# A two-layer mixture-of-experts encoder: overflow tiles in mid-stream, expert pairs across groups, ten early gathers and five late

## Time and profile before

| | us |
|---|---|
| median of three runs (1248.49 to 1252.61) | 1248.56 |
| the profiled execution, its own time | 1249.58 |
| its span in the trace | 1247.7 |
| TensorE busy, in the span | 1062.6 (85%) |
| VectorE, ScalarE, GpSimd busy | 492.1, 294.1, 269.7 |

### The profile page before, as it was taken

How to read it: one execution, slowest core, us unless ns; L and a number is a source line. 1 busy time by engine, 2 the same in 40 slices (tenths; PEclk the granted TensorE clock), 3 DMA queues, 4 the chain that set the end, 5 groups by cost and what they waited for, 6 DMA issues and landing times.

```text
span 1247.7 us, 14600 instructions
## 1 busy us (share of the span) xinstructions
PE 1062.6 (85%) x5342; PEld 620.7 (50%) x5342; DVE 492.1 (39%) x1075; ACT 294.1 (24%) x631; POOL 269.7 (22%) x289
## 2 busy tenths in 40 slices
PE   6999999999997898887774998988987998877870
PEld 5777777775455333333223776754545333333320
DVE  3144444435347211111115699996455111111116
ACT  3233232323110111000012455546111010000012
POOL 2000000001000321111033388870003121111033
PEclk9999999999997999989996999999997998999995
DMA  8963222411806899999984293100028999999974
GB/s 274 386 200 112 95 75 71 117 58 58 353 24 264 309 419 421 420 420 421 421 324 120 57 374 97 34 16 9 34 101 309 415 420 421 420 420 420 419 274 133
DMA packets 110287, 303.68 MB, mean 243 GB/s; under 512 B 18440, under 2 KB 65672, under 8 KB 86521
## 3 DMA queue, kind: packets, MB, share of 16 engines
q1 hardware_dynamic: 87977, 254.74, 53.0%
q0 software_dynamic: 22256, 48.22, 10.7%
HBM read 278.34 MB, written 57.12 MB: 269 GB/s over the span
## 4 chain that ended last, share of the span: by engine, by line
PE 52%; DMA 20%; issue 11%; DVE 10%; ACT 2%; POOL 2%; another core or an unknown queue 1%; SPq 1%; DVEq 0%; POOLq 0%
PE bank L541 10%; DMA ring<-in_w_up 10%; PE bank L1234 10%; DMA arena<-in_w_up 8%; PE bank L440 7%; PE bank L1253 6%; PE bank L568 4%; DVE bank L1763 3%; PE bank L591 2%; PE bank L607 2%; PE bank L632 2%; PE bank L1223 1%; PE bank L973 1%; POOL ring L1191 1%; PE bank L348 1%
## 5 line engine op out<-in xcount | busy, mean ns | idle before, releaser
L1234 PE MATMUL bank<-ring,work 128*64 128x512 f32 x704 | 166.1, 627 | 28.4 <-DMA ring<-in_w_up 26.6
L1253 PE MATMUL bank<-ring,work 128*64 128x512 f32 x528 | 126.7, 624 | 28.7 <-DVE work L1272 21.7
L541 PE MATMUL bank<-arena,ring 128*128 128x288 f32 x512 | 131.9, 412 | 0.3 <-issue 0.3
L1549 PE MATMUL bank<-arena,work 128*128 128x288 f32 x512 | 126.6, 410 | 5.7 <-DMA work<-in_w_pw 4.4
L1268 DVE TENSOR_TENSOR work<-work,bank 128x256 f32<-128x256 f32 x33 | 13.9, 421 | 283.8 <-ACT work L1264 276.3
L1234 PEld LDWEIGHTS bank<-ring,work 128*64 128x64 f32 x704 | 57.9, 144 | 134.3 <-issue 132.2
L1549 PEld LDWEIGHTS bank<-arena,work 128*128 128x128 f32 x512 | 98.1, 192 | 33.5 <-issue 4.9
L1712 POOL TENSOR_TENSOR ring<-ring 128x606 f32<-128x606 f32 x76 | 103.6, 1364 | 43.6 <-ACT ring L1660 34.1
L541 PEld LDWEIGHTS bank<-arena,ring 128*128 128x128 f32 x512 | 94.9, 190 | 32.9 <-issue 8.2
L440 PE MATMUL bank<-ring,arena 128*128 128x512 f32 x224 | 99.1, 595 | 2.6 <-ACT arena L1696 2.6
L1234 PE MATMUL bank<-arena,work 128*64 128x512 f32 x352 | 85.6, 642 | 18.4 <-DMA arena<-in_w_up 16.2
(11 more groups left out here) (262 smaller groups left out, 1330.9 us busy)
## 6 DMA issues: line engine op xcount, KB each, us to landing
ring<-in_w_down SPq DMA_DIRECT2D x32, 2048.0 KB, 24.0
ring<-in_w_gate SPq DMA_DIRECT2D x20, 2048.0 KB
ring<-in_w_up SPq DMA_DIRECT2D x20, 2048.0 KB
arena<-in_w_gate SPq DMA_DIRECT2D x10, 2048.0 KB
arena<-in_w_up SPq DMA_DIRECT2D x8, 2048.0 KB
ring<-in_w_qkv SPq DMA_DIRECT2D x24, 512.0 KB, 6.0
y_sorted<-gain POOLq DMA_DIRECT2D x8, 1536.0 KB, 5.7
work<-in_w_pw SPq DMA_DIRECT2D x16, 512.0 KB, 5.8
```

The source lines that it names most:

```text
L541: mm = nc.tensor.matmul(bank[b][:, 0:HT], wa[s][:, w, c, :], xt[:, c, h * HT:(h + 1) * HT], start=c == 0, stop=c == C - 1)
L1234: mm = nc.tensor.matmul(bank[2 + s][rr, :], rows_t[:, c, rr], wgu[g][:, :, e, c, :], start=c == 0, stop=c == C - 1)
L1253: mm = nc.tensor.matmul(bank[5 + h][rr, :], hts[:, c, rr], wdn[s][:, e, c, h * HALF:(h + 1) * HALF], start=c == 0, stop=c == FC - 1)
L1549: mm = nc.tensor.matmul(bank[banks[h][w]][:, 0:GT], wp[s][:, w, c, :], xt[:, c, h * GT:(h + 1) * GT], start=c == 0, stop=c == C - 1)
```

```diff
...
+        y_early = [ring[:, 1, n % EARLY_BUFS * D:(n % EARLY_BUFS + 1) * D] for n in range(2 * TILES)]
+        y_late = [ring[:, 0, j * D:(j + 1) * D] for j in range(TILES)]
...
+        OVER_AT = EPAIRS // 2
+        LAST_SLOT = 2
+        def gu_at(p):
+            if p == EPAIRS - 1:
+                return LAST_SLOT
+            return (p if p < OVER_AT else p + 1) % GU_SLOTS
...
-                do(V.tensor_tensor(grouped(kept), grouped(le), pen[0:r, :].unsqueeze(2).to_broadcast([r, GROUPS, PER_GROUP]),
+                do(V.tensor_tensor(placed_at(kept), grouped(le), pen[0:r, :].unsqueeze(2).to_broadcast([r, GROUPS, PER_GROUP]),
...
+            FAR = float(2 * SLOTS)
+            do(V.tensor_scalar(late_is[:], slot_f[:], float(EARLY_PAIRS * P), None, ALU.is_ge))
+            do(V.scalar_tensor_tensor(late_is[:], slot_f[:], float(EXPERTS * CAP), late_is[:], ALU.is_lt, ALU.mult))
+            do(V.scalar_tensor_tensor(early_slot[:], late_is[:], float(ZERO_ROW), slot_f[:], ALU.mult, ALU.max))
+            do(V.scalar_tensor_tensor(far_f[:], late_is[:], -FAR, slot_f[:], ALU.mult, ALU.add))
+            do(V.tensor_tensor(far_f[:, 0, :], far_f[:, 0, :], far_f[:, 1, :], ALU.min))
+            do(V.tensor_scalar(late_slot[:], far_f[:, 0, :], FAR, None, ALU.add))
...
+                if local == EARLY_PAIRS:
+                    pool.wait_ge(base.gu_mm, i + 1)
+                    for j in range(TILES):
+                        steps.done(pool.memset(y_late[j], 0.0))
+                    pool.wait_ge(further_known, 2 * (l + 1))
+                    pool.wait_ge(over_end, l + 1)
+                    for s in range(2):
+                        pool.wait_ge(base.y_out[s], 16 * (EPAIRS // 2) * (l + 1))
+                    g, there = gu_slot(l, EPAIRS - 1)
+                    pool.wait_ge(base.gu_in[g], there)
+                    early_rows_in(pool, l, range(0, FIRST_EARLY))
                 pool.wait_ge(base.y_ev_a, i + 1 + FREE)
                 pool.wait_ge(base.y_ev_d, i + 1 + FREE)
                 rows_out(local)
                 if local == EARLY_PAIRS:
...
-                        for k in range(2):
...
-                                y_rows_in(pool, j, k, early_slot)
...
+                    early_rows_in(pool, l, range(FIRST_EARLY, 2 * TILES))
+        FIRST_EARLY = 2
...
+        def early_rows_in(pool, l, some):
+            for n in some:
+                j, k = n // 2, n % 2
+                if n >= EARLY_BUFS:
+                    pool.wait_ge(early_sum, TILES * l + (n - EARLY_BUFS) // 2 + 1)
+                pool.indirect_dma_start(y_early[n][0:rows[j], :], None, y_sorted,
+                                        bass.IndirectOffsetOnAxis(early_slot[0:rows[j], k, j:j + 1], 0),
+                                        bounds_check=SLOTS, oob_is_err=False).then_inc(gathered[j], 16)
+        def late_pool(pool, l):
             for s in range(2):
                 pool.wait_ge(base.y_out[s], 16 * (EPAIRS // 2) * (l + 1) + 16)
-            pool.wait_ge(extra_end, l + 1)
             for j in range(TILES):
...
-                for k in range(2):
-                    y_rows_in(pool, j, k, late_slot if early(j, k) else slot)
+                pool.indirect_dma_start(y_late[j][0:rows[j], :], None, y_sorted,
+                                        bass.IndirectOffsetOnAxis(late_slot[0:rows[j], j:j + 1], 0),
+                                        bounds_check=SLOTS - 1, oob_is_err=False).then_inc(late_in[j], 16)
+        def early_dve(dve, steps, l, j):
+            r = rows[j]
+            dve.wait_ge(gathered[j], 32 * (l + 1))
+            steps.done(nc.vector.scalar_tensor_tensor(x[0:r, j, :], y_early[2 * j][0:r, :], gate_w[0:r, 0, j:j + 1],
+                                                      x[0:r, j, :], ALU.mult, ALU.add))
+            nc.vector.scalar_tensor_tensor(x[0:r, j, :], y_early[2 * j + 1][0:r, :], gate_w[0:r, 1, j:j + 1],
+                                           x[0:r, j, :], ALU.mult, ALU.add).then_inc(early_sum, 1)
         def combine_dve(dve, steps, l, j):
             r = rows[j]
-            dve.wait_ge(gathered[j], landed(j, l + 1))
-            steps.done(nc.vector.scalar_tensor_tensor(x[0:r, j, :], y_at[0][j][0:r, :], gate_w[0:r, 0, j:j + 1],
...
+            dve.wait_ge(early_sum, TILES * l + j + 1)
+            dve.wait_ge(late_in[j], 16 * (l + 1))
+            nc.vector.scalar_tensor_tensor(x[0:r, j, :], y_late[j][0:r, :], late_gate[0:r, 0, j:j + 1],
                                            x[0:r, j, :], ALU.mult, ALU.add).then_inc(combined, 1)
...
+                if local == OVER_AT:
+                    over_turns(eng, l, over)
...
+            def over(o):
+                act.wait_ge(m.xt_mm, o + 1)
+                nc.scalar.copy(over_xt, bank[7][:].rearrange("p (c r) -> p c r", c=C)).then_inc(m.xt_ev, 1)
+                act.wait_ge(m.gu_mm, o + 1)
+                nc.scalar.activation(over_hid, bank[7][0:CAP, 0:FE], ACT.Silu).then_inc(m.silu, 1)
+                act.wait_ge(m.dn_mm, o + 1)
+                nc.scalar.copy(over_y, bank[7][:]).then_inc(m.y_ev, 1)
+                act.wait_ge(m.y_ev, o + 1 + FREE)
+                for h in range(2):
+                    act.dma_start(y_sorted[dyn(EXPERTS * CAP + o * CAP, CAP), h * HALF:(h + 1) * HALF],
+                                  over_y[h * CAP:(h + 1) * CAP, :]).then_inc(m.y_out, 16)
...
+                if local == EPAIRS - 1:
+                    early_dve(dve, steps, l, 0)
                 ex_y_copy(dve, nc.vector.tensor_copy, base, i, s, k, 1, base.y_ev_d)
...
+                if local == EPAIRS - 1:
+                    for j in range(1, TILES):
+                        early_dve(dve, steps, l, j)
...
+        def of_pair(src, l, p):
+            return src[l].rearrange("(g e) d f -> e g d f", g=GROUPS)[p // 2, 2 * (p % 2):2 * (p % 2) + 2]
...
                 i = EPAIRS * l + local
-                down_first = local >= GU_SLOTS
-                if 0 < local and local + GU_SLOTS < EPAIRS and not down_first:
+                gu = lambda p: gu_load(sp, l, p)
+                late = local in (OVER_AT - 2, OVER_AT - 1, EPAIRS - 3)
+                if 0 < local < GU_SLOTS or late:
                     sp.wait_ge(base.gu_mm, i + 1)
-                    gu_load(sp, l, local + GU_SLOTS)
+                    gu(local + 2 if late else local + GU_SLOTS)
                 if local + 2 < EPAIRS:
                     sp.wait_ge(base.dn_mm, i + 1)
+                    if local == OVER_AT:
+                        sp.wait_ge(m.y_out, 32 * tiles + 32)
+                        sp.sem_inc(over_end, 1)
+                        gu(local + 2)
                     dn_load(sp, l, local + 2, local % 2)
-                if local + GU_SLOTS < EPAIRS and down_first:
-                    gu_load(sp, l, local + GU_SLOTS)
...
+                if local == OVER_AT - GU_SLOTS:
+                    over_loads()
+                elif local >= GU_SLOTS and local + GU_SLOTS < EPAIRS - 1 and not late:
+                    gu(local + GU_SLOTS)
+            m = overs[l]
+            def over_load(o):
+                sp.dma_start(over_x, x_over[dyn(o * CAP, CAP), :]).then_inc(m.x_in, 16)
+                expert = sp.value_load(over_expert[0:1, dyn(o, 1)], min_val=0, max_val=EXPERTS - 1)
+                for w, src in enumerate((w_gate, w_up)):
+                    sp.dma_start(over_gu[:, w, :, :].rearrange("p c f -> p (c f)"),
+                                 src[l, dyn(expert, 1)].rearrange("e (p c) f -> p (e c f)", c=C)).then_inc(m.gu_in, 16)
+                sp.dma_start(over_dn.rearrange("p c n -> p (c n)"),
+                             w_down[l, dyn(expert, 1)].rearrange("e (p c) n -> p (e c n)", c=FC)).then_inc(m.dn_in, 16)
+            def over_loads():
+                sp.sem_inc(m.y_out, 32)
+                with sp.If(tiles > 0):
+                    sp.wait_ge(far_scattered, 16 * (2 * TILES - FAR_FIRST) * (l + 1))
+                    over_load(0)
+                with sp.If(tiles > 1):
+                    with sp.Fori(1, tiles) as o:
+                        sp.wait_ge(m.dn_mm, o)
+                        sp.wait_ge(m.y_out, 32 * o + 32)
+                        over_load(o)
...
-                extra_loads(0)
...
-            sp.wait_ge(gathered[HALF_TILES - 1], landed(HALF_TILES - 1, 1))
+            sp.wait_ge(late_in[HALF_TILES - 1], 16)
...
```

242 lines of the change are left out of this document (104 added, 138 removed).

## The result

The changed kernel takes 1238.86 us (median of 8 runs, 1237.70 to 1239.12), the kernel before 1248.1 (8 runs, 1243.35 to 1252.61). The ratio is 0.9933, 95% interval 0.9917 to 0.9949: faster by 0.67%, some 8.4 us, where 15 were forecast. The profiled execution took 1239.12 us, its span is 1237.5.

What follows compares the result with a forecast made beforehand. Weight streams at 419 to 421 GB/s bound the kernel, with chains of waits at both layer ends. 1249.58 − 4.7 (layer 0) − 10.8 (layer 1) + 0.4 gave 1234.5 us profiled, 1233.5 median; range 1228.5 to 1241.0.

Steps and rivals of the forecast that it cites:

- (1): Layer 0's end: pair 15's store issued 0.3 us later and landing 1.2 later behind more gathers; together +1.5 us.
- they need gathers 0 and 1 within 10.4 us: Tile 0's early sums, ahead of pair 15's output copy, cost nothing if those gathers land by 648.2 us.
- (2): Layer 0, last store's landing to first late sum: 5.98 us down to 3.86, so −2.1.
- (6): Layer 1, last store's landing to first late sum: 5.35 us down to 3.86, so −1.5.
- (3): Layer 0, first late sum to first GLU product: 16.33 us down to 12.2, so −4.1.
- (4): Layer 1: overflow tile moved into the stream, 3.67 MB at 420 GB/s, delays all behind it by 8.7 us.
- (5): Layer 1's end: last store lands at 1212 to 1219 us against 1218.84; −3.5 us, bounds −6 and 0.
- (7): Layer 1, first late sum to last norm's end: 20.1 us before, five sums fewer, so −5.8.
- Between the layers: Small router operations, 0.2 us a layer; +0.2 forecast from layer 0's first GLU product to layer 1's pair 0.
- A: Rival, chance 0.20: last store slow behind ten gathers, 1240.3 us. Stage: layer 0, pair 15 to first GLU product.
- C: Rival, chance 0.03: gather issues wait for VectorE's sums, 1246.4 us. Stage: layer 1, pair 0 to pair 15.
- D: Rival, chance 0.05: layer 1's stream starves; over 0.5% slower needs 41 us turn. Stage: pair 15 to last norm's end.

## Why the prediction was right and where it was not

The range and the sign held; the size was 15 where 8 to 9 came. The largest mis-sized terms are the landing to the first sum (2.8 us over both layers), the first sum to the first product (1.7) and the tile's bytes (1.5). Against the terms of the sum:

- **(1) Layer 0's store.** I had its issue 0.3 late, 14.9 us behind pair 15's start. It was 17.6. The step "they need gathers 0 and 1 within 10.4 us" did not quite hold: tile 0's sum started at 647.99 and pushed the output copy to 650.51; and I had not added that gathers 8 and 9 wait for that sum (651.39) and stand ahead of the store (653.90). That it landed at 660.91 (7.01 after its issue, by the chain of waits), only 0.5 later after pair 15's start than before, was the one-engine list's doing, which I had seen and priced as a small extra instead of as what ends last. Against that landing of before (24.1), the repeats of the changed kernel lie at 24.6 to 26.6, and my +1.5 lies among them by luck: the late issue was hidden behind a list that I had not let decide.
- **(2) and (6) Landing to first sum**, forecast 3.86 at both ends. It was 5.0 (660.91 to 665.92) and 5.5 (1214.92, which is 6.57 behind the issue by the chain of waits, to 1220.44). The step that failed is "one late gather instead of two", with its 1.32 us. In layer 0 SP's turn did go (landing to issue 1.71 to 0.84 us), in layer 1 there was nothing to lose (1.03, now 1.06). And the first gather alone needs 4.2 and 4.5 us from issue to sum, about what two took before (4.27 and 4.32). Its issue took 1.73 us at both ends, against 1.00 before; where it took 1.0, in layer 1 of the runs with few warm-up products and with the weights later, it needed 3.7 and 3.8. So one gather for two is worth some 0.5 us, and a longer issue takes that back.
- **Why that issue took longer.** Rows of VectorE and GpSimd show it together. Tile 4's early sum of 661.31 ends at 662.58, and the issue that began inside it, at 661.75, ends at 663.48, 0.90 later. Over the ends of both layers in the fourteen traces, 180 issues began while VectorE was in a sum or in the scaling of a norm (L1245, L1247, L1254 and L363 here); 175 of them ended 0.80 to 0.98 us after that operation did, and the other 5, begun within 0.1 us of its start, took 0.94 to 0.99. The 272 that began outside of one took 0.94 to 1.04, also the 45 during which one started. So an issue waits for the sum that runs when it begins, up to 1.2 us, and for no later one.
- **(3) First sum to first product**: 13.9, forecast 12.2. My list of VectorE and ScalarE left out TensorE's warm-up products (to 671.9, tile 0 normed at 670.2) and put tile 2's Square ahead of the copies of tile 0, where ScalarE's order has it behind. With both set right it is 11.7, and the forecast 12.2.
- **(4) The tile's bytes**, 8.7: C grew by 10.2. The turn itself took 13.1 us from its first transposes to its last product, 14.4 forecast, and SP's queue had work throughout. The slow spot accounts for the rest: 5 us at 247 instead of 415 GB/s are 2.0 us. No row of before showed it.
- **(5) Pair 15 to landing in layer 1**: 21.8 us (20.2 to 21.8 over the repeats), forecast 22.1 from the up weights. The number is right and one reading under it is not: the earlier trace rows pools 22 stores of both layers, most of them issued with the weight stream in front, so it says nothing of gathers. Here the store landed 6.6 us after its issue, below the 7.8 that I took as the least. The 1.5 us of latency in the sum stand in no row; a store with little in front of it landed in 2.7 and 2.9 us (the kernel before without its tile).
- **(7) The norms**: 20.1 to 13.7, forecast 14.3. Right.
- **Between the layers** I had +0.2, and B grew by 2.5 in the profiled pair. That is mostly the granted clock at 850 us: 0.72 in the changed kernel's window above, 1.00 in the kernel before and in the run with few warm-up products (second row):

```profile
850.00:856.00 6.00, 3.38 (x11) 1.54 (x10) 5.90 (x10) 4.83 (x10) 0.00 (x0) 1.00 0.00 0
...
850.00:856.00 6.00, 4.25 (x10) 2.01 (x11) 5.97 (x13) 5.80 (x11) 0.00 (x0) 1.00 0.00 0
```

All fourteen profiled executions fall into two groups by it. Where the clock stays at 1.00 there, B is 271.0 in the kernel before and 271.3 to 272.0 in the changed versions; where it falls, B is 272.7 and 272.7 in the kernel before and 272.8 to 273.6 in the changed ones. At like clock the change costs some 0.3 us here, near the +0.2. The clock fell in both repeats of the kernel before, and in all seven executions of the changed kernel and its versions with the same warm-up products; it stayed up in the four versions with other ones. Why it falls was not tested.

Of the prediction's rivals, A's mechanism (a held copy, a late issue) came true at its place in layer 0, with 3 us instead of 0.7, and its landing did not. A's time has a slip: 3.1 instead of 1.2 and the copy's 0.7 make layer 0 2.6 worse, not 1.6, so A ends at 1241.3, just outside the range that was to hold it. C's mechanism is there, and I had read its rows wrongly. Of the two issues that I compared, the one of 0.99 us began before the first sum (1224.19 to 1225.47) and ran on beside it; the one of 1.26 began inside that sum, at 1225.08, and ended at 1226.34, 0.87 after it. That is a full wait for the running sum, not a slowdown of 0.3 at most. C's price of 1.31 us for each of eight sums was wrong too, since an issue waits for one sum alone: it cost 0.7 at the first late gather of both layers. D never came near. Two of my signs for a wrong forecast did appear: the output copy that waits for tile 0's sum, and the slice below 410 GB/s.

What stays open: whether it is the number of rows or the half of the partitions that makes the 64-row load slow, since the one edit changed both; why the granted clock falls at 850 us in some executions; and what the pairs and gathers give apart from the tile's move.

## What to carry to other kernels

Ask of each store and gather not only when it is issued but what stands last in each engine's queue; where two things hold the same landing, taking one away showed nothing or 2 us, and both together 5. When work moves off the end, the price of the end is what it disturbs there too: here the tile's loads slowed a store that had nothing to do with it. And follow the list of every engine through a shortened stage, the warm-up products and the order of ScalarE's copies too, since the stage only shrinks to the next one of them. Before explaining 2 us in a stage, look at the same stage in other executions of unchanged work: here A, B and D each moved by about that much by themselves.

## What the runs showed of the hardware

- With a load of 64 rows of 4 KB to 64 partitions in flight among weight loads in rows of 8 KB, full queues moved 247 GB/s over 5 us (254 in the second execution of the same kernel); with 128 rows to 128 partitions or without it, in one execution each, the engines moved 419 to 421 in that slice.
- A load of 31 rows of 4 KB went through one engine, at 25 to 29 GB/s, and a store issued 20 to 24 us later waited for it; as 16 and 15 rows it held the store 2 us less, and with the store issued first 5 us less.
- GpSimd's issue of an indirect DMA took 0.94 to 1.04 us. Begun inside a sum of VectorE, it ended 0.80 to 0.98 us behind that sum, up to 2.08 us in all (175 of 180 such issues); a sum that started during an issue did not lengthen it (45 issues).
- TensorE's transposes (8 of 128x128) took 1.97 us at a granted clock of 0.50 (1.2 GHz) and 1.16 at 1.00 (2.4 GHz). The clock was at 0.50 behind 18 us in which TensorE idled, rose to 1.00 at 673 us behind the ten warm-up products, at 679 with four, and at 667, ahead of the transposes, with 24 that started 5 us sooner.
